# One-hot stage of a routed-expert layer: weighted rows divided among VectorE, ScalarE and GpSimd

## The reference

```
ids = take_along_axis(cand_i, f_pos)          # (T, 8 heads, 16): row * 128 + column of a 128 x 128 grid of experts
g   = softmax(f_s)                            # (T, 8, 16), the weights
u = take(u_tab, ids);  v = take(v_tab, ids)   # (T, 128, 1024) each
a = gelu(einsum('tkd,td->tk', u, x))
out = einsum('tk,tkd->td', g * a, v)
y = layer_norm(ALPHA * x + gate2 * out)
```

```
G[t, column, row] = sum_p  (column_p == column) * weight_p  *  (row_p == row)
```

## Time and profile before

| | us |
|---|---|
| median of 2 runs | 3667.28 (3666.48 to 3668.08) |
| the profiled execution | 3670.94 |
| its span | 3669.2 |
| mean granted TensorE clock | 0.964 of full speed |
| PE busy | 3393.6 (92%) |
| DVE busy | 2638.0 (72%) |
| ACT busy | 1270.7 (35%) |
| POOL busy | 1323.4 (36%) |

### The profile page before, as it was taken

One profiled execution on the slowest core, in us unless ns is written; L12 is line 12 of the kernel. 1 busy time (PEld: TensorE's weight loads), 2 busy tenths in 40 slices (PEclk: granted clock), 3 DMA queues, 4 the chain that ended last, 5 costly groups with the idle time before them and its releaser, 6 DMA issues.

```text
span 3669.2 us, 46914 instructions
## 1 busy us (share of the span) xinstructions
PE 3393.6 (92%) x17312; PEld 2803.2 (76%) x17312; DVE 2638.0 (72%) x5343; ACT 1270.7 (35%) x2399; POOL 1323.4 (36%) x828
## 2 busy tenths in 40 slices
PE   8888899999999846999999999999999999999996
PEld 3455446666667745899998999989889999999995
DVE  0122114666777898788888988878998888888865
ACT  1222123333333258333333333333333333333332
POOL 1000000488886000577776333223333322333202
PEclk9998899999999879999999999999999999999998
DMA  9200353566655424999999999999889999999943
GB/s 399 109 13 14 127 201 131 158 158 153 155 151 166 167 92 202 357 355 360 353 347 320 366 344 366 344 346 341 340 328 357 361 350 355 342 356 356 356 171 122
DMA packets 270174, 952.87 MB, mean 260 GB/s; under 512 B 74234, under 2 KB 127610, under 8 KB 210690
## 3 DMA queue, kind: packets, MB, share of 16 engines
q1 hardware_dynamic: 154466, 521.75, 38.4%
q0 software_dynamic: 115200, 428.07, 33.1%
q10 hardware_dynamic: 288, 0.16, 0.0%
HBM read 888.70 MB, written 61.18 MB: 259 GB/s over the span
## 4 chain that ended last, share of the span: by engine, by line
PE 51%; DVE 6%; DMA 2%; issue 1%; ACT 1%; SPq 0%; POOLq 0%; POOL 0%; ACTq 0%; DVEq 0%
PE bank L1541 26%; PE bank L1555 25%; DMA vw<-in_v 2%; DVE ring L1643 1%; DVE accS L1660 1%; DVE uL L1721 1%; DVE vL L1716 1%; ACT vR L1606 0%; DVE ga L1736 0%; DVE cL L1713 0%; DVE slots L1698 0%; DVE st L1689 0%; DVE slots L1686 0%; DVE slots L1672 0%; DMA uw<-in_u 0%
## 5 line engine op out<-in xcount | busy, mean ns | idle before, releaser
L1502 POOL DMA_INDIRECT ring<-in_uv,slots x384 | 587.9, 1531 | 1253.8 <-DVE accS L1660 1009.7
L143 POOL DMA_INDIRECT g_cells<-slots x384 | 665.8, 1734 | 387.4 <-DVE slots L1205 257.0
L1541 PE MATMUL bank<-hR,uR 128*128 128x384 f32 x2048 | 693.4, 339 | 42.1 <-DVE uL L1721 42.1
L1541 PE MATMUL bank<-hR,uL 128*128 128x384 f32 x2048 | 692.5, 338 | 0.0
L1541 PE MATMUL bank<-hL,uR 128*128 128x384 f32 x2048 | 691.4, 338 | 0.0
L1660 DVE SCALAR_TENSOR_TENSOR accS<-ring,cs,accS 128x1024 f32<-128x1024 f32 x381 | 489.5, 1285 | 13.6
L1555 PE MATMUL bank<-vR,cR 128*128 128x512 f32 x1536 | 477.5, 392 | 0.7 <-DVE slots L1672 0.7
L1555 PE MATMUL bank<-vR,cL 128*128 128x512 f32 x1536 | 476.0, 391 | 0.0
L1555 PE MATMUL bank<-vL,cR 128*128 128x512 f32 x1536 | 475.7, 391 | 0.0
L1643 DVE CUSTOM_DVE_ANT_0 ring<-ring,slots 128x1024 f32<-128x1024 f32 x384 | 460.3, 1236 | 0.1
L1600 ACT ACTIVATE cR<-ga 128x384 fp32r<-128x384 f32 x256 | 134.5, 525 | 930.4 <-PE bank L1555 776.0
(11 more groups left out here) (233 smaller groups left out, 3913.9 us busy)
## 6 DMA issues: line engine op xcount, KB each, us to landing
uw<-in_u SPq DMA_DIRECT2D x256, 512.0 KB, 6.0
vw<-in_v SPq DMA_DIRECT2D x256, 512.0 KB, 6.9
wr<-in_w_pq SPq DMA_DIRECT2D x36, 2048.0 KB, 8.7
wr<-in_w_o SPq DMA_DIRECT2D x18, 2048.0 KB, 8.5
g_cells<-free POOLq DMA_DIRECT2D x32, 768.0 KB, 7.1
g_blocks<-stage SPq DMA_DIRECT2D x12, 2048.0 KB, 6.3
gw<-g_blocks SPq DMA_DIRECT2D x32, 768.0 KB, 13.6
gw<-g_cells SPq DMA_DIRECT2D x32, 768.0 KB, 8.8
```

Source lines behind the costliest of these rows:

```text
L143: pool.indirect_dma_start(out=g_dram[1][:, :], out_offset=bass.IndirectOffsetOnAxis(ap=slots[:, i, D + k:D + k + 1].bitcast(U32), axis=0), ...
L1502: pool.indirect_dma_start(out=ring[:, k % R, :], out_offset=None, in_=a["uv"], in_offset=bass.IndirectOffsetOnAxis(ap=ids[:, k // P, k % P ...
L1541: mm = pe.matmul(A[t][:, 0:CW], w[:, t, k, :], h[:, k, :], start=(k == 0 and w is uR and h is hR), stop=(k == DK - 1 and w is uL))
```

## The change

Three engines make the weighted rows of a unit's eight tokens: ScalarE the first UA = 2 (from `e2`, as before), VectorE the next UD = 2, GpSimd the last UP = 4. VectorE and GpSimd make theirs in one fused instruction per token, `(iob == column index) * weight`, with the index and the weight read as one value per partition; they no longer go by `e2`. So `e2` shrinks to two tokens (128 x 256). The column index is also cast to f32 (`idf`, double-buffered), one more instruction of VectorE per tile. A new semaphore `pool_cb` counts GpSimd's units; TensorE waits for it before the second half of a unit only. VectorE no longer waits for `hot`. The comparison `ra` and the products are as they were.

```
+    UA, UD, UP = 2, 2, 4
...
+        idf = sb(c, "idf", [P, 2, P])
+        e2 = sb(c, "e2", [P, 2, UA, P], BF16)
...
             def _(pool):
                 pool.iota(iob[:, :], pattern=[[1, P]], base=0, channel_multiplier=0,
                           allow_small_or_imprecise_dtypes=True).then_inc(const, 1)
+                pool.wait_ge(const, 1)
+                for d in range(len(DT)):
+                    pool.wait_ge(w_ev, d + 1)
+                    pool.wait_ge(idx_ev, d + 1)
+                    for x in range(NU):
+                        n = d * NU + x
+                        if n >= 2:
+                            pool.wait_ge(sc_mm, 2 * (n - 1))
+                        for k in range(U - UP, U):
+                            t = x * U + k
+                            ins = pool.tensor_scalar(cb[:, n % 2, k, :], iob[:, :], idf[:, d % 2, t:t + 1],
+                                                     wf[:, d % 2, 1, t:t + 1], ALU.is_equal, ALU.mult)
+                        ins.then_inc(pool_cb, 1)
...
                         for e in range(2):
                             f = 2 * n + e
+                            if e:
+                                pe.wait_ge(pool_cb, n + 1)
...
                     if d >= 2:
                         act.wait_ge(row_ready, NU * (d - 1))
+                        act.wait_ge(pool_cb, NU * (d - 1))
...
-                        for k in range(UD, U):
+                        for k in range(UA):
                             ins = act.activation(cb[:, n % 2, k, :], e2[:, n % 2, k, :], ACT.Copy,
...
                     if d >= 2:
                         dve.wait_ge(cb_ready, NU * (d - 1))
+                        dve.wait_ge(pool_cb, NU * (d - 1))
...
+                    dve.tensor_copy(idf[:, d % 2, :], part[:, 1, :])
...
-                        dve.tensor_tensor(e2[:, n % 2, :, :], io,
-                                          at[:, 1, :].rearrange("p (t o) -> p t o", o=1).to_broadcast([P, U, P]),
+                        dve.tensor_tensor(e2[:, n % 2, :, :], io.to_broadcast([P, UA, P]),
+                                          at[:, 1, 0:UA].rearrange("p (t o) -> p t o", o=1).to_broadcast([P, UA, P]),
                                           ALU.is_equal).then_inc(hot, 1)
...
-                        dve.wait_ge(hot, n + 1)
-                        dve.tensor_tensor(cb[:, n % 2, 0:UD, :], e2[:, n % 2, 0:UD, :],
-                                          wf[:, d % 2, 1, x * U:x * U + UD].rearrange("p (t o) -> p t o", o=1).to_broadcast(
-                                              [P, UD, P]), ALU.mult).then_inc(row_ready, 1)
+                        for k in range(UA, UA + UD):
+                            t = x * U + k
+                            ins = dve.tensor_scalar(cb[:, n % 2, k, :], iob[:, :], idf[:, d % 2, t:t + 1],
+                                                    wf[:, d % 2, 1, t:t + 1], ALU.is_equal, ALU.mult)
+                        ins.then_inc(row_ready, 1)
```

More of the change, by code:

```diff
@@ L1239, in weigh @@
         ra = sb(c, "ra", [P, 2, U, P])
-        e2 = sb(c, "e2", [P, 2, U, P], BF16)
+        idf = sb(c, "idf", [P, 2, P])
+        e2 = sb(c, "e2", [P, 2, UA, P], BF16)
         cb = sb(c, "cb", [P, 2, U, P])
         const, chain, idx_mm, idx_ev, w_ev = (sem(f"r_{n}") for n in ("const", "chain", "idxmm", "idxev", "wev"))
-        hot, row_ready, cb_ready, sc_mm, st_ev = (sem(f"r_{n}") for n in ("hot", "row", "cb", "scmm", "stev"))
+        hot, row_ready, cb_ready, pool_cb, sc_mm, st_ev = (sem(f"r_{n}") for n in (
+            "hot", "row", "cb", "pool", "scmm", "stev"))
         st_out = [sem(f"r_stout{k}") for k in range(2)]
@@ L1249, in weigh @@
         BU = TB // U
-        UD = 3
         with nc.Block() as block:
@@ L1359, in _ @@
                         at = idxb[:, d % 2, :, x * U:(x + 1) * U]
-                        io = iob[:, :].rearrange("p (o k) -> p o k", o=1).to_broadcast([P, U, P])
-                        dve.tensor_tensor(e2[:, n % 2, :, :], io,
-                                          at[:, 1, :].rearrange("p (t o) -> p t o", o=1).to_broadcast([P, U, P]),
+                        io = iob[:, :].rearrange("p (o k) -> p o k", o=1)
+                        dve.tensor_tensor(e2[:, n % 2, :, :], io.to_broadcast([P, UA, P]),
+                                          at[:, 1, 0:UA].rearrange("p (t o) -> p t o", o=1).to_broadcast([P, UA, P]),
                                           ALU.is_equal).then_inc(hot, 1)
-                        dve.tensor_tensor(ra[:, n % 2, :, :], io,
+                        dve.tensor_tensor(ra[:, n % 2, :, :], io.to_broadcast([P, U, P]),
                                           at[:, 0, :].rearrange("p (t o) -> p t o", o=1).to_broadcast([P, U, P]),
                                           ALU.is_equal)
-                        dve.wait_ge(hot, n + 1)
-                        dve.tensor_tensor(cb[:, n % 2, 0:UD, :], e2[:, n % 2, 0:UD, :],
-                                          wf[:, d % 2, 1, x * U:x * U + UD].rearrange("p (t o) -> p t o", o=1).to_broadcast(
-                                              [P, UD, P]), ALU.mult).then_inc(row_ready, 1)
+                        for k in range(UA, UA + UD):
[3 more added lines that the diff above has]
+                        ins.then_inc(row_ready, 1)
 def experts(nc, a, sb, sem, PS, slots, x1_dram, g_dram, gate_dram, placed):
```

## The result

The changed kernel takes 3733.68 us (median of 2 runs, 3733.49 to 3733.88) against 3667.28: 66 us or 1.85% longer, ratio 1.0185 with a 95% interval of 1.016 to 1.0209. The interval lies on both sides of 2% slower. The forecast was 3675, with 3735 as the upper end of its range; the sign was right, the size was eight times too small. The profiled execution took 3733.88, its span 3732.1.

What follows compares the result with a forecast made beforehand. VectorE was taken to bound the stage at 2.74 us a unit; in turns, VectorE's 1.5 plus GpSimd's 1.4 gave 2.9, so 48 x 0.16 = 7.7 us plus 0.4 for casts: 3675 us, range 3636 to 3735.

Steps and rivals of the forecast that it cites:

- What bounds the kernel before: In this stage, which stands alone, VectorE sets the pace at 2.74 us a unit, 48 units.
- VectorE by itself: VectorE's work per unit in the stage falls from 2.74 to 1.97 us, 37 us less if that were everything.
- GpSimd by itself: GpSimd's four fused instructions take 0.35 us each, 1.4 us a unit (1.1 to 2.2), fitting beside VectorE's 1.97.
- GpSimd beside VectorE: Both engines strictly take turns in the new loop: 1.5 plus 1.4 gives 2.9 us a unit against 2.74.
- the price bounds: GpSimd's instruction between 0.282 and 0.54 us, taking turns with VectorE: 3662 to 3711 us, chance 0.45.
- rival 3: GpSimd's instruction is dear, 0.8 us, so a unit takes 4.7 us: +94 us, 3761 us; chance 0.15.
- The rule on VectorE's fused instructions: If VectorE's fused instructions (bf16 in, f32 out) do not contend with GpSimd, a unit is 2.74 us, no change.
- the dear instruction: Same as rival 3: GpSimd's instruction costs 0.8 us, a unit 4.7 us, +94 us; chance 0.15.
- Rivals 1 and 2: GpSimd's turns short and partly hidden, 3651 us, chance 0.22; no collision worth naming, VectorE alone at 1.97, 3631 us, chance 0.15.
- rival 1: GpSimd holds the shared path only some 0.2 us per instruction; unit 2.4 us, -16 us, 3651 us; chance 0.22.
- The signs named beforehand: Right if `ra` lasts well over 1.21 us; wrong if blocking is rare or GpSimd's undisturbed duration lies outside 0.28 to 0.54.

Runs made afterwards that it cites:

- run 7: Changed kernel without GpSimd's loop and its waits, split ScalarE 5, VectorE 3 by fused instructions: 3662.61 us, ratio 0.999 to the kernel before.
- runs 4 and 10: Changed kernel, GpSimd making 64 of 128 columns: 3688.52 us; and, with VectorE's numbers in PSUM, GpSimd only multiplying an f32 row by a constant: 3641.40 us.
- run 5: Changed kernel with the row of numbers that VectorE's comparisons read in PSUM (f32) instead of SBUF (bf16), same output: 3688.14 us.
- run 3: Changed kernel with GpSimd's four instructions only comparing, without the multiplication and its per-partition scalar: 3692.09 us.

## Why the prediction was wrong

- *What bounds the kernel before* was right: the stage stands alone, and a unit that lasts 1.42 us longer appears 48-fold in the time.
- *VectorE by itself* was right. `e2` of 256 columns costs 0.34 to 0.35 from start to start (1420.13 to 1420.48) against 0.32 forecast; run 7, whose VectorE terms use the same slope and the same 0.26 for a fused instruction, took 2.64 for 2.65.
- *GpSimd by itself* is the step that failed. The prediction took 0.35 us with 0.54 as the upper end; it is 0.77. The lower end rested on a select of 0.282 us, another kind of instruction; the upper end put a fixed 0.10 under the columns, by a memset that reads nothing, where runs 4 and 10 point to 0.33 and show 0.53 for the plainest tensor-scalar; and no term stood for the second operation (0.19 with its scalar). The two scalars cost 0.07, under the 0.115 of the upper end. This term alone is 4 x 0.42 x 48 = 81 us.
- *GpSimd beside VectorE* failed in the form it was given. The rows of 1024-column sums showed strict turns with each side waiting. With instructions of 128 columns on GpSimd's side, only one direction kept its full price: `ra` never waited in the changed kernel (1208 to 1221 ns) and `e2` in three units of 48. The cost was no sum of what both hold, but GpSimd's four instructions plus one wait of about 1.08 us: 3.08 + 1.08 = 4.16, not 1.5 + 3.08 = 4.6. This takes back 0.42 x 48 = 20 us. The forecast's 8 plus 81 less 20 is 69; measured are 66. The two errors partly cancel. That the time still fell 1.3 us inside the range is luck: the price bounds ended at 3711, and only the piece of rival 3 that was let in reached 3735.
- The rule on VectorE's fused instructions, which the text left open, came out small: they cost GpSimd 0.1 us a unit (run 5, where no comparison holds it up), and two of them lasted 0.74 us in the changed kernel's steady state against 0.60 in run 5.
- Of the rivals, the dear instruction (0.8 us, 3761 us, chance 0.15) had the right price, and its sign came: TensorE waits for GpSimd while VectorE stands idle. Its time was too long because it used the same sum of turns. Rivals 1 and 2 fell with the price; but rival 1's picture, a GpSimd instruction that holds VectorE off for some 0.2 us only, is near what run 3 shows (0.11 us + 0.10 us of waiting).
- The signs named beforehand served: the durations of `ra` well over 1.21 did not come, and GpSimd's undisturbed duration outside 0.28 to 0.54 did.

TensorE was granted 0.75 to 0.83 of its clock in stretches between 1360 and 1460 us, where the kernel before had 1.00 in most; it waits for GpSimd there all the same, and GpSimd waited for TensorE only 1.7 us in the whole stage, so nothing of the time is put down to it. Why a tensor-scalar of GpSimd has a fixed price of some 0.3 to 0.5 us stays open; no run here looks inside it.

## What to carry to other kernels

Before work is moved to an idle engine, time one such instruction there: an engine that is free is not one that is fast, and rows of another kind of instruction bound nothing. A comparison of VectorE with two SBUF inputs stops a GpSimd instruction that starts while it runs until it ends, and mostly through a second one that follows without a gap; with one of the inputs in PSUM it does not, at no cost to VectorE. Divide by the measured prices only after that collision is out: the same split (4, 2, 2) was 0.4% slower than the kernel before with it, and 0.5% faster without.

## What the runs showed of the hardware that was not expected

- GpSimd's tensor-scalar on 128x128: 0.77 us from start to start with two operations and two per-partition scalars, 0.70 with constants, 0.58 with one operation and one scalar, 0.55 for 64 columns, 0.49 (0.528 in the record) for one multiplication by a constant; f32 or bf16 input makes no difference.
- The exclusion between the two engines is lopsided for short GpSimd instructions. One that started within a comparison went from 0.79 to 1.86 us (behind `e2` of 256 columns and `ra`), and to 2.31 behind `e2` of 512 columns and `ra`. A comparison that started 0.11 us into one of GpSimd's waited 0.10 us (run 3), and one that started 0.49 us into it did not wait.
- A 128x1024 comparison with one operand broadcast from PSUM took 1.215 us, as with both in SBUF (1.218).
